# Joining the two maps of a differential head on VectorE before they are turned and weighted

## The reference, cut to what matters

```python
o = causal_block_attention(q, k, v, DIFF_HEAD_DIM ** -0.5)       # (B, S, heads, 2 maps, 128)
lam = exp(sum(lv[0] * lv[1])) - exp(sum(lv[2] * lv[3])) + lam_init
o = o[:, :, :, 0, :] - lam * o[:, :, :, 1, :]
o = rmsnorm(o, out_gain) * (1.0 - lam_init)
```

## Time and profile before

| what | value |
|---|---|
| median of three runs | 3071.86 us (3069.78 to 3079.41) |
| span of the profiled execution, first to last instruction | 3063.9 us |
| what lies around the span, taken as the median less the span | 8.0 us |
| PE busy | 2817.8 us, 92% of the span |
| DVE busy | 1173.5 us, 38% |
| ACT busy | 740.2 us, 24% |
| POOL busy | 1978.0 us, 65% |
| mean granted TensorE clock | 0.965 of 2.4 GHz |
| diff stretch of the first layer, first scores to last finish | 349.5 to 454.3 us |
| diff stretch of the second layer | 1513.4 to 1618 us |

### The profile page before, as it was taken

How to read it: one execution, slowest core, us unless ns; L and a number is a source line. 1 busy time by engine, 2 the same in 40 slices (tenths; PEclk the granted TensorE clock), 3 DMA queues, 4 the chain that set the end, 5 groups by cost and what they waited for, 6 DMA issues and landing times. The chain is left out here.

```text
span 3063.9 us, 38961 instructions
## 1 busy us (share of the span) xinstructions
PE 2817.8 (92%) x14268; PEld 2290.0 (75%) x14268; DVE 1173.5 (38%) x1944; ACT 740.2 (24%) x1421; POOL 1978.0 (65%) x1602
## 2 busy tenths in 40 slices
PE   6988999999899997988999999899998999989997
PEld 5766787778788886766777778788887776777775
DVE  4377364211210114178173320310112496436773
ACT  3220454100120202231365110120111214212250
POOL 5867421788698895867520888698886771366604
PEclk9998999999999998999999999999998999999998
DMA  4312100233223333322100223233234320142201
GB/s 123 93 52 68 45 8 11 79 94 96 72 94 97 96 96 81 106 62 69 50 8 1 80 86 97 69 96 97 94 99 92 83 78 20 32 99 67 76 1 69
DMA packets 158903, 217.27 MB, mean 71 GB/s; under 512 B 51312, under 2 KB 62832, under 8 KB 158704
## 3 DMA queue, kind: packets, MB, share of 16 engines
q1 hardware_dynamic: 119952, 209.72, 23.3%
q10 hardware_dynamic: 38752, 4.95, 1.3%
HBM read 212.52 MB, written 2.10 MB: 70 GB/s over the span
## 5 line engine op out<-in xcount | busy, mean ns | idle before, releaser
L290 POOL TENSOR_TENSOR weight_parts<-weight_ring,zero 128x512 fp32r<-128x512 f32 x760 | 863.4, 1136 | 872.6 <-PE ps L375 457.8
L293 POOL TENSOR_TENSOR weight_parts<-weight_ring,weight_parts 128x512 fp32r<-128x512 f32 x780 | 1075.1, 1379 | 62.8 <-ACT weight_parts L301 2.5
L377 PE MATMUL ps<-h_feature_major_high,weight_parts 128*128 128x512 f32 x2304 | 587.8, 395 | 20.3 <-DVE h_feature_major_low L471 6.6
L377 PEld LDWEIGHTS ps<-h_feature_major_high,weight_parts 128*128 128x128 f32 x2304 | 432.7, 190 | 126.8 <-issue 12.5
L375 PE MATMUL ps<-weight_parts,h_feature_major_high 128*128 128x512 f32 (+1 forms) x1920 | 458.3, 378 | 34.3 <-DVE h_feature_major_low L1641 9.1
L375 PEld LDWEIGHTS ps<-weight_parts,h_feature_major_high 128*128 128x128 f32 x1920 | 338.3, 192 | 117.6 <-issue 21.7
L377 PE MATMUL ps<-h_feature_major_low,weight_parts 128*128 128x512 f32 x1152 | 311.2, 392 | 0.0
L375 PE MATMUL ps<-weight_parts,ut_high 128*128 128x512 f32 x1024 | 254.6, 390 | 0.0
L377 PEld LDWEIGHTS ps<-h_feature_major_low,weight_parts 128*128 128x128 f32 x1152 | 218.5, 190 | 46.4
L375 PE MATMUL ps<-weight_parts,h_feature_major_low 128*128 128x512 f32 (+1 forms) x960 | 237.8, 374 | 0.0
L375 PEld LDWEIGHTS ps<-weight_parts,ut_high 128*128 128x128 f32 x1024 | 191.6, 188 | 42.3 <-POOL weight_parts L293 1.7
(11 more groups left out here) (239 smaller groups left out, 3077.6 us busy)
## 6 DMA issues: line engine op xcount, KB each, us to landing
weight_ring<-in_w_in SPq DMA_DIRECT2D x344, 256.0 KB, 2.7
weight_ring<-in_w_mlp SPq DMA_DIRECT2D x256, 256.0 KB, 2.7
weight_ring<-in_w_out SPq DMA_DIRECT2D x64, 256.0 KB, 2.6
weight_ring<-in_w_mem_kv SPq DMA_DIRECT2D x32, 256.0 KB, 2.9
weight_ring<-in_w_diff_o SPq DMA_DIRECT2D x32, 256.0 KB, 2.6
weight_ring<-in_w_mla_o SPq DMA_DIRECT2D x16, 256.0 KB, 2.6
weight_ring<-in_w_cross_o SPq DMA_DIRECT2D x16, 256.0 KB, 2.6
arena<-in_mem SPq DMA_DIRECT2D x2, 1024.0 KB, 5.4
```

What stands on the lines that cost most here:

```text
L290: self.nc.gpsimd.tensor_tensor(high, raw, self.m["zero"][:].broadcast_to([P, raw.shape[1]]), ALU.add).then_inc(self.s["slab_high"], 1)
L293: self.nc.gpsimd.tensor_tensor(low, raw, high.bitcast(F32), ALU.subtract).then_inc(self.s["slab_split"], 1)
L377: last = self.nc.tensor.matmul(banks[:, t, :], w[:, cut], h, **ends)
```

## The change

In a diff unit a new DVE step, join(u), stands between exp and turn. It takes both reciprocals, forms lam_neg * sum0 / sum1 in a column, and adds the second map times that column to the first, in place, over all n keys. turn then transposes only map 0, and the bank alternates between 4 and 5 with u, so that turn(u) of two neighbouring diff units waits for copy(u-2) and not copy(u-1). copy takes one map out, weight multiplies one map, and finish is one instruction that scales the one product by the first reciprocal. DVE runs join with a lag of one round: maximum(i), join(i-1), finish(i-3). turn waits for join in place of exp. Cross, mla and second-stack units keep their steps.

```diff
+    def joins(self, u):
+        return self.units[u]["kind"] == "diff"
+    def turned_banks(self, u):
+        return [(0, 4 + u % 2)] if self.joins(u) else [(0, 4), (1, 5)]
...
     def turn(self, u):
         pe, a = self.nc.tensor, self.units[u]
-        pe.wait_ge(self.s["exped"], u + 1)
+        if self.joins(u):
+            pe.wait_ge(self.s["joined"], sum(map(self.joins, range(u + 1))))
+        else:
+            pe.wait_ge(self.s["exped"], u + 1)
         if u >= 1:
-            pe.wait_ge(self.s["turned_copied"], u)
-        for j in range(2):
+            pe.wait_ge(self.s["turned_copied"], u - 1 if self.joins(u) and self.joins(u - 1) else u)
+        for j, bank in self.turned_banks(u):
...
-                dst = self.m["ps"][0:width, 4 + j, kb:kb + P]
+                dst = self.m["ps"][0:width, bank, kb:kb + P]
...
     def weight(self, u):
-        for j in range(2):
+        for j, _ in self.turned_banks(u):
...
     def copy(self, u):
-        act.activation(self.m["probs_t"][0:rows, u % 2, :, 0:width], self.m["ps"][0:rows, 4:6, 0:width],
+        turned = self.turned_banks(u)
+        first, maps = turned[0][1], len(turned)
+        act.activation(self.m["probs_t"][0:rows, u % 2, 0:maps, 0:width], self.m["ps"][0:rows, first:first + maps, 0:width],
                        ACT.Copy).then_inc(self.s["turned_copied"], 1)
...
+            def join(u):
+                n, r, total = units[u]["n"], m["recip"][:, u % 8, :], m["rowsum"][:, u % 8, :]
+                dve.wait_ge(s["exped"], u + 1)
+                v.reciprocal(r, total)
+                v.drain()
+                v.tensor_scalar(r[:, 1:2], r[:, 1:2], total[:, 0:1], lam_neg, ALU.mult, ALU.mult)
+                v.drain()
+                first, second = (m["probs"][:, u % 2, j, 0:n] for j in range(2))
+                v.scalar_tensor_tensor(first, second, r[:, 1:2], first, ALU.mult, ALU.add).then_inc(s["joined"], 1)
...
             def finish(u):
-                v.reciprocal(r, m["rowsum"][:, u % 8, :])
-                v.drain()
                 if a["kind"] == "diff":
-                    dst = od[:, i, p2 * P:(p2 + 1) * P]
-                    v.tensor_scalar(dst, sums[:, P:2 * P], r[:, 1:2], lam_neg, ALU.mult, ALU.mult)
-                    v.drain()
-                    v.scalar_tensor_tensor(dst, sums[:, 0:P], r[:, 0:1], dst, ALU.mult, ALU.add).then_inc(s["finished"], 1)
+                    v.tensor_scalar(od[:, i, p2 * P:(p2 + 1) * P], sums[:, 0:P], r[:, 0:1], None, ALU.mult).then_inc(s["finished"], 1)
                     return
+                v.reciprocal(r, m["rowsum"][:, u % 8, :])
+                v.drain()
...
-            A.steps(U1, U2, (0, A.maximum), (3, finish), between=dict(zip(prep_rounds, pieces)))
+            A.steps(U1, U2, (0, A.maximum), (1, join), (3, finish), between=dict(zip(prep_rounds, pieces)))
```

More of the change, by code:

```diff
@@ L227 @@
     "outs_ready", "gated", "merging_done", "merged_high", "merged",
-    "scores", "maxed", "exped", "turned", "turned_copied", "weighted", "finished",
+    "scores", "maxed", "exped", "joined", "turned", "turned_copied", "weighted", "finished",
     "index_scores", "index_relu", "index_added",
```

## The result

The changed kernel takes 3079.31 us (median of ten runs, 3075.61 to 3082.41), the kernel before 3071.34 us beside it (ten runs, 3067.44 to 3079.41): a ratio of 1.0024, 95% interval 1.0012 to 1.0035. It is slower by 8 us, within the 0.3% that was called no change. The forecast was 3079 us.

The account below looks back on a forecast made before the run. PE sets the pace, with DVE full beside it in five heads of eight. A layer: early +7.9, late -7.6, POOL +2, clock +1.5, so +3.8; both +7.6. Span 3071.5 plus 8.0 gives 3079 us, range 3064 to 3096.

Parts of the forecast that it names:

- VectorE's early sum: Up to the maximum of unit 28, M(28): joins add 20.1 us, shorter finishes remove 12.2, so +7.9 us a layer.
- the column product: In the join, one column times two pointer scalars on VectorE: 0.28 us taken, bounds 170 ns and 410 ns.
- the join's sum by n: The join's scalar_tensor_tensor adding the two maps on VectorE: pitches of 0.27, 0.41, 0.54, 0.67 us by n.
- Late part: Units 28 to 39: heads of 10.1 us, 1.9 less than today, and a shorter end; -7.6 us a layer.
- POOL +2: Joins reading two SBUF inputs slow down beside POOL's work: +2 us a layer, bounds 0 and 4.7.
- the two waits: In late heads PE waits for the join before turns T(256) and T(128): 0.97 and 0.54 us.
- The clock, +1.5: PE idles in rounds with a preparation piece and its clock falls: +1.5 us a layer, bounds 0 and 6.
- rival 3: Joins meet POOL each time, clock falls in most rounds with a piece: +11 us a layer, 3094 us; chance 0.24.
- The 8.0 us around the span: Time outside the profiled span, added to the forecast span of 3071.5 us to give 3079 us.
- Rival 1: PE sets the end and DVE keeps up: -53 us, 3018 us; chance 0.04.
- Rival 2: Late heads without PE waits, 8.6 us each, no POOL or clock cost: -4.2 us a layer, 3063.5 us; chance 0.13.

Follow-up runs that it names:

- the filler run: Changed kernel with four idle 128x128 matmuls on PE while it waits for the join, units 8 to 27: 3074.10 us, ratio 1.0013 to the kernel before.

## Why the prediction was right, point by point

- **The median, 3079.31 against 3079, is closer than the reasoning, and that is luck.** I forecast +3.8 us a layer; the two profiled executions show +7.5 and +4.6, and the ratios of two sets of runs (1.0024, 1.0026) say 3.7 to 4 a layer. The mechanism held, and terms of either sign were off.
- **VectorE's early sum, +7.9.** Right: M(28) came at 423.47, the early part grew by 10.0 and 9.4, and with the clock held up by filler by 6.9. The prices it was made of stand: 0.27 us for the column product (0.28 taken), 0.35 to 0.75 us for the join's sum by n, 0.34 for finish. The heads are another matter: I gave 13 to 14.5 us to an early head, and from one 512 maximum to the next they take 12.3 to 16.0, with a mean of 14.0.
- **Late part, -7.6 and POOL +2.** The step was right, its size less so. A head without pieces and POOL takes 9.9 us, not 10.1, and the two waits are 0.98 and 0.69. Without POOL's products the late part is 6.3 us shorter than before, with a cold clock in part of it. With them it is 2.5 to 4.8 us shorter. By these parts POOL costs 1.5 to 3.8 us where I took 2 with bounds of 0 and 4.7; by whole stretches 0.8 to 3.8, and the times allow less than 2.
- **The clock, +1.5.** Mis-sized: 2.4 to 3.1 us a layer by the filler run, within the bounds of 0 and 6. I had reckoned that work at 1.2 GHz in a round that VectorE sets costs 0.4 us a time, from PE's mean of 2.15 us a round. The round with the weight step and the scores of a 512 unit holds much more (the rows from 366.69 on, over 5 us at the low clock), and behind it VectorE waited 1.37 us. The granted clock of the early part, 0.85 and 0.90, reached but did not pass 0.85, the mark I had set for rival 3.
- **The 8.0 us around the span** were 2.2 us, as said above; that error and the too small rise of the stretch nearly cancel in the sum of the median. The forecast span was 3071.5 us, and the profiled one was 3078.5.
- **Rival 1** (PE sets the end, 3018 us): what it describes is seen once VectorE's work or the pieces are gone (3028 and 3035 us). By the Trainium skill, "Perfetto Trace Analysis", Identifying the Most-Contended Engine, the engine with the highest occupancy is optimised first, and the headroom of TensorE is judged by MFU and weight-load share. PE was that by either of its rows, 92% busy with matmuls and 75% with weight loads against POOL's 65%, and making it 29 us less busy made the kernel 8 us slower. The measurement decides: in an early head two engines were full.
- **Rivals 2 and 3.** Rival 2 is out: late heads do wait, 0.98 and 0.69 us. Rival 3 had the right costs in mind and too much of each: clock and POOL add 3 to 7 us a layer, not 11, and the column product is not dearer than I took it (0.27 us).
- **POOL and the two-input join.** The Trainium skill, "SBUF — State Buffer", Who interferes with whom, calls the port pair that VectorE and GpSimd share "an exclusive lock" and has the order of issue decide who waits. The trace agrees: a join of 0.75 us took 1.96 beside a product of 1.5 us. It goes either way: at 376.84 a pair of POOL's copies took 1.84 us in place of 1.28 beside a join that kept its 0.75.

## What to carry to other kernels

Before work is moved off a busy engine, sum the receiving engine over the slice where it will land, with all that is scheduled there, and not over the kernel: 1.0 us of VectorE a unit turned 18 us saved a layer into 5 to 7 lost. The same change made only where the receiver has room gave the stretch back 4 us a layer, and the same test tells how large a saving was to be had. Where the engine that is relieved is TensorE, its new idle time has a price of its own through the clock.

## What was not expected of the hardware

- Useless matmuls made the changed kernel some 5 us faster: 80 more a layer in PE's waits took the ratio from 1.0026 to 1.0013 and the granted clock of the early part from 0.85 to 0.90 up to 0.97.
- Two executions of one program had stretches of 108.4 and 105.4 us, each the same in both layers to 0.03 us, at mean clocks of 0.87 and 0.94. A profile's length of one stretch can carry 3 us that the next profile doesn't.
